# Seven places of split weights, 4128 bytes apart instead of 4096

## The chip, the core and the metric

One core of a Trainium2 chip runs the whole program. The metric is the device time of one execution in microseconds (us). Three executions of the kernel before took 2169.74, 2171.64 and 2173.57 us; the median, 2171.64 us, is the time to compare with.

## What is computed

Two transformer stacks in a row on 256 tokens of width 1024, all in float32. The first puts 16 meta tokens ahead (272 tokens) and has two layers of: half a SwiGLU feed-forward block (width 2816), a mixer (four retention heads and four differential attention heads) and another half feed-forward block. The second has two layers of feed-forward, mixer, feed-forward, where the mixer is a gated short convolution in layer 0 and dilated attention with three groups of 16 heads in layer 1. Cut to what matters here:

```python
h = h + 0.5 * (silu(rmsnorm(h) @ w_gate) * (rmsnorm(h) @ w_up)) @ w_down   # eight of these
h = h + mixer(rmsnorm(h) @ w_in) @ w_out                                    # four of these
```

Nearly all of the work is the product of a weight matrix, read once from memory, with activations of 256 or 272 columns (tokens).

## The kernel before

**Split products.** To keep float32 accuracy in TensorE's faster float32 format (fp32r), each operand is split in a high part, the value rounded to fp32r, and a low part, the difference. A product takes three matmuls: high weights by high activations, high weights by low activations, low weights by high activations. They are issued in the helper `matmuls` (L1658): the first at L1685, the second at L1686, the third at L1687. Where high and low activations lie one behind the other with 256 columns each (the feed-forward stages behind the first stack's second mixer), the first two are one matmul of 512 columns (L1683), and L1687 follows it. `project_first` (L1698, matmuls at L1702) does the same for the first six tiles. `values` (L2014, matmuls at L2025 to L2027) turns the roles round: the activations are the stationary operand, and the weights of three neighbouring places are the moving one, 3 by 128 columns.

**The weights' way.** SyncE's queue loads each unit of weights (L683, mostly 1024 rows by 256 columns) into one of four raw buffers, `raw`. ScalarE copies half a unit, [128 partitions, 8, 128], into a place of `whi` (L836, `highs`; the first six at L1152); VectorE subtracts this from the raw values into the same place of `wlo` (L1178, `lows`; the first six at L1636). Both tensors have seven places (`NP = 7`), and one place is 8 x 128 x 4 = 4096 bytes of every partition. `Plan` (L235) fixes ahead which tile of weights goes to which place: the one that was last used longest ago (L318), but for three neighbouring places kept for `values`. There are 728 tiles of weights. ScalarE fills a place again when the matmuls of its last tile are done (`plan.spent`), VectorE follows ScalarE (semaphore `hi`), and TensorE follows VectorE (`lo`, L1676). All this runs up to several tiles ahead.

**Where the operands lie.** The allocator puts the buffers of a partition one behind the other, each at a multiple of 32 bytes. `raw`, `whi`, `wlo`, `h` and `x` have sizes that are multiples of 256 bytes, so every place of `whi` and `wlo`, and the start of `x` and of `a`, is at the same byte mod 256; call it byte 0. Counted so, these are the starts of the moving operands:

| stages (index) | operand | columns | start, byte mod 256 |
|---|---|---|---|
| 0 to 3: feed-forward, mixer, feed-forward, feed-forward; 4: the tiles with 272 columns | `x`, `a` | 272 | 0 and 128 (high), 64 and 192 (low), by turns over k |
| 1: mixer, output | `y` | 272 | 32 and 96 to 224, by turns |
| 4: second mixer, query tiles | `x` from column 16 | 256 | 64 and 192 (high), 128 and 0 (low) |
| 5, 6, 8, 9, 11: feed-forward | `x_close`, `a_close` | 512 and 256 | 32 |
| 4 (output), 7, 10 | `y_close`, `x_close`, `c_yy`, `d_y` | 256 | 32 |

The 32 comes from `HALF_LINE = 8` elements in `close` (L552), and where that is 0, from what lies ahead of the buffer. One step over k inside a place is 128 x 4 = 512 bytes, two times 256.

The order of everything on the engines is written out by hand or by the plan; none of it depends on addresses.

Of the kernel before, what the change touches and what calls it, by code (L numbers as in the profile page):

```python
# [11 lines left out]
F32R = mybir.dt.float32r  # L12
# [3 lines left out]
P = 128  # L16
# [10 lines left out]
NP = 7  # L27
AHEAD = 6

HALF_LINE = 8  # L30
NH = 16
NSEG = 9

# [408 lines left out]
def build(nc, A, out):  # L442
    ctx = ExitStack()
    names = [0]

    def alloc(c, shape, dt=F32):
        names[0] += 1
        return c.enter_context(nc.sbuf_tensor(f"t{names[0]}", shape, dt))
# [3 lines left out]

    with ctx:
        raw = alloc(ctx, [P, NRAW, 8, PAIR])
        whi = alloc(ctx, [P, NP, 8, P], F32R)
        wlo = alloc(ctx, [P, NP, 8, P], F32R)
        h = alloc(ctx, [P, KC, T])
        x = alloc(ctx, [P, KC, 2, T], F32R)
        acc = alloc(ctx, [P, T])
# [19 lines left out]
        with block1:  # L479
# [4 lines left out]
            with region:  # L484
# [6 lines left out]
                rb = alloc(region, [33, 48])  # L491
                eb = alloc(region, [NH, NSEG * P])
                lam = alloc(region, [64, 16])
# [46 lines left out]
        ps = ctx.enter_context(nc.psum_tensor("ps", [P, 8, 512], F32))  # L540
        scr = nc.dram_tensor("bias_rows", [NH, NSEG * P], F32, kind="Internal")
        bands = nc.dram_tensor("bias_bands", [NH, P, 2, NKEY], F32, kind="Internal")

# [8 lines left out]
        def close(t, n, first):  # L552

            whole = t[:, :, :, :].rearrange("p k m c -> p (k m c)")
            return whole[:, first:first + n * 2 * SEQ].rearrange("p (k m c) -> p k m c", k=n, m=2)

        x_close, a_close, y_close = close(x, KC, HALF_LINE), close(a, FCH, HALF_LINE), close(y, KC, 0)

        raw_first = raw[:, 0:3, :, :].rearrange("p r k n -> p (r k n)").rearrange(
            "p (k u c) -> p k u c", k=KC, u=2)  # L560
# [130 lines left out]
        def _(pool):  # L691
# [21 lines left out]
            def mixer(s):  # L713
                l, cq = mix_of[s], STAGES[s][1]

                def rotate(kind, i, n):

                    c0, q = cq if kind in ("dq", "rq") else 0, 1 if kind in ("dq", "dk") else 0
                    v, row, turned = n % 2, ROW[kind] + i, sh[:, n % 2, 0:T - c0]
                    w.wait_ge(S["shuf"], 16 * l + n + 1)  # L720
                    pool.tensor_tensor(turned, turned, rotr[:, 2 * q + 1, c0:T], ALU.mult).then_inc(S["spun"], 1)
                    w.wait_ge(S["spun"], 16 * l + n + 1)
                    w.wait_ge(S["evac"], T0[s] + MIX_TILES.index((kind, i)) + 1)
                    pool.tensor_tensor(qk[:, row, c0:T], m1[:, v, 0:T - c0], turned, ALU.add).then_inc(S["qk"], 1)

                def low_y(kind, i, c):
                    w.wait_ge(*of_head("yh", l, kind, i))
                    hi, lo = (mixed_of(s)[:, c, m, 0:T - cq] for m in range(2))
                    pool.tensor_tensor(lo, yv[:, cq:T] if kind == "d" else qk[:, i, cq:T], f32(hi), ALU.subtract).then_inc(S["yl_" + kind], 1)

                def step(what, i):
                    if what == "O2":
                        low_y("d", i, 4 + i)
                    elif what == "R5":
                        low_y("r", i, i)

                n = 0
                for k, (kind, i) in enumerate(MIX_TILES):
                    if kind in ROW:
                        rotate(kind, i, n)  # L740
                        n += 1
                    for what, head in steps_at(k, True) + steps_at(k, False):
                        step(what, head)
                for n in sorted(OUT_STEPS):
                    for what, head in OUT_STEPS[n]:
                        step(what, head)
# [29 lines left out]
            mixer(plan.mixers[0])  # L776
            for n in range(NH):

# [11 lines left out]
            s = STAGES.index((DIL, META, W_FFN2 + 8))  # L790
            w.wait_ge(S["bands"], 16 * 8 * NH)

            w.wait_ge(S["evac"], T0[s])

            def bias(n):
                if n >= 2:
                    w.wait_ge(S["hmax"], n - 1)
                pool.dma_start(d_bias[:, n % 2, :, :], bands.ap()[n]).then_inc(S[f"bias{n % 2}"], 16)

            def stack_values(b):  # L800

                w.wait_ge(S["evac"], T0[s] + NT * b + NT)
                for half in range(2):
                    for g in range(2):
                        pool.dma_start(d_v12[64 * g:64 * g + 64, b % 2, half:4:2, :],
                                       d_vk[64 * half:64 * half + 64, b % 2, :, 1 + g, :]).then_inc(S["stacked"], 16)
# [3 lines left out]
            for b in range(KC):  # L810
                stack_values(b)
                for n in range(2 * b + 2, min(2 * b + 4, NH)):
                    bias(n)
# [1295 lines left out]
```

## Time and profile before

| | |
|---|---|
| median of three runs | 2171.64 us |
| the profiled execution: its time | 2173.17 us |
| the profiled execution: its span, first to last instruction | 2171.1 us |
| TensorE, matmuls | 2158.2 us busy (99%) |
| TensorE, weight loads (beside the matmuls) | 2039.8 us (94%) |
| VectorE | 1558.4 us (72%) |
| ScalarE | 1220.8 us (56%) |
| GpSimd | 458.1 us (21%) |
| DMA | 395.35 MB at a mean of 182 GB/s |

Busy time of TensorE counts a matmul from its start to its modelled end, and matmuls overlap. What sets the pace is the distance from one start to the next, and this has to be read from start times: over n starts, (last start - first start) / (n - 1).

### The profile page before, as it was taken

Reading aid. Unit: us, or ns where it says so; the run is one execution under the profiler, and the core shown is the slowest. Engines: PE = TensorE matmul, PEld = TensorE weight load, DVE = VectorE, ACT = ScalarE, POOL = GpSimd, SP = SyncE. Lnnn points to the kernel's source line nnn. Section 1 sums busy time; section 2 is a strip of 40 time slices with the busy share of each in tenths; the row PEclk is TensorE's granted clock in tenths of the full one; section 3 lists DMA queues with packets and bytes.
Section 4 is the critical chain, followed back from the end, with each engine's and each line's share of the span. In section 5 each row is a group of like instructions: output and inputs, shape, how many; then the busy total and the mean of one; then the engine's idle time right before and its main releaser. Section 6 shows DMA issues by size and latency. Waiting matters only on the chain.

```text
span 2171.1 us, 38708 instructions
## 1 busy us (share of the span) xinstructions
PE 2158.2 (99%) x15614; PEld 2039.8 (94%) x15614; DVE 1558.4 (72%) x2588; ACT 1220.8 (56%) x2017; POOL 458.1 (21%) x499
## 2 busy tenths in 40 slices
PE   9999999999999999999999999999999999999999
PEld 9999999999999999988988999889888999999888
DVE  8655977665665586876697586975876688887863
ACT  6444466444544456665566444655655576676652
POOL 1000522420350052231053000430331011101420
PEclk9999999999999999999999999999999999999999
DMA  8655435975786543565466554755555576674653
GB/s 279 206 165 174 152 118 147 240 191 166 197 208 183 174 156 117 172 198 194 155 213 204 186 185 147 230 193 192 181 190 177 168 198 173 175 230 141 225 178 106
DMA packets 424082, 395.35 MB, mean 182 GB/s; under 512 B 16816, under 2 KB 420400, under 8 KB 423905
## 3 DMA queue, kind: packets, MB, share of 16 engines
q1 hardware_dynamic: 410336, 375.22, 55.1%
q0 software_dynamic: 13280, 17.33, 3.8%
q8 instruction: 124, 2.03, 0.4%
q14 instruction: 54, 0.43, 0.1%
q10 hardware_dynamic: 288, 0.34, 0.0%
HBM read 389.20 MB, written 7.41 MB: 183 GB/s over the span
## 4 chain that ended last, share of the span: by engine, by line
PE 93%; DVE 3%; ACT 2%; DMA 1%; issue 1%; SPq 0%; ACTq 0%
PE ps L1687 29%; PE ps L1683 25%; PE ps L1685 16%; PE ps L1686 16%; DMA t<-attn_w_qkv 1%; DVE t L1178 1%; PE ps L2027 1%; PE ps L2026 1%; PE ps L2025 1%; PE ps L1702 1%; PE ps L1803 0%; PE ps L1848 0%; PE ps L1977 0%; DVE t L1213 0%; PE ps L1993 0%
## 5 line engine op out<-in xcount | busy, mean ns | idle before, releaser
L1687 PE MATMUL ps<-t 128*128 128x256 f32 (+1 forms) x5456 | 1548.2, 284 | 0.0
L1687 PEld LDWEIGHTS ps<-t 128*128 128x128 f32 x5456 | 1029.2, 189 | 0.1
L1178 DVE TENSOR_TENSOR t<-t 128x1024 fp32r<-128x1024 f32 (+1 forms) x722 | 876.4, 1231 | 174.5 <-ACT t L836 174.0
L1685 PE MATMUL ps<-t 128*128 128x272 f32 (+1 forms) x3036 | 876.2, 289 | 0.2 <-DVE t L1405 0.2
L836 ACT ACTIVATE t<-t 128x1024 fp32r<-128x1024 f32 (+1 forms) x722 | 729.9, 1030 | 256.7 <-PE ps L1687 229.1
L1686 PE MATMUL ps<-t 128*128 128x272 f32 (+1 forms) x3036 | 866.0, 285 | 0.0
L1683 PE MATMUL ps<-t 128*128 128x512 f32 x2420 | 840.2, 390 | 0.0
L1685 PEld LDWEIGHTS ps<-t 128*128 128x128 f32 x3036 | 571.5, 188 | 5.9 <-issue 3.4
L1686 PEld LDWEIGHTS ps<-t 128*128 128x128 f32 x3036 | 574.4, 189 | 0.9
L1683 PEld LDWEIGHTS ps<-t 128*128 128x128 f32 x2420 | 454.1, 188 | 95.0
L760 POOL TENSOR_TENSOR t<-t 128x256 f32<-128x256 f32 x110 | 100.6, 914 | 694.2 <-ACT t L954 694.2
L944 ACT ACTIVATE t<-ps 128x256 f32<-128x256 f32 x220 | 83.1, 378 | 132.4 <-PE ps L1687 132.4
L783 POOL DMA_DIRECT2D bias_bands<-bias_rows x128 | 104.2, 821 | 217.3 <-PE ps L1687 165.3
L753 POOL TENSOR_TENSOR t<-t 128x256 fp32r<-128x256 f32 x110 | 129.6, 1178 | 9.4 <-ACT t L937 9.4
L851 ACT ACTIVATE t<-t 128x256 fp32r<-128x256 f32 (+1 forms) x95 | 49.7, 531 | 91.8 <-DVE t L1263 83.2
L974 ACT ACTIVATE t<-t 128x272 fp32r<-128x272 f32 x66 | 28.5, 432 | 115.5 <-DVE t L1358 115.5
L1213 DVE SCALAR_TENSOR_TENSOR t<-ps,t 128x512 f32<-128x512 f32 (+2 forms) x52 | 28.6, 551 | 80.4 <-ACT t L879 80.1
L937 ACT ACTIVATE t<-t 128x256 fp32r<-128x256 f32 x110 | 45.6, 415 | 66.9 <-DVE t L1328 66.9
L1324 DVE TENSOR_TENSOR t<-ps,t 128x256 f32<-128x256 f32 x110 | 46.7, 424 | 48.9 <-ACT t L944 45.8
L1317 DVE TENSOR_TENSOR t<-ps,t 128x256 f32<-128x256 f32 x110 | 46.2, 420 | 43.6 <-ACT t L944 42.9
L1328 DVE TENSOR_TENSOR t<-t 128x256 f32<-128x256 f32 x110 | 71.0, 645 | 0.0
L1355 DVE TENSOR_TENSOR t<-ps,t 128x272 f32<-128x272 f32 x66 | 29.1, 440 | 50.7 <-PE ps L1687 50.7
(200 smaller groups left out, 1560.1 us busy)
## 6 DMA issues: line engine op xcount, KB each, us to landing
t<-ffn_w_in SPq DMA_DIRECT2D x88, 1024.0 KB, 5.3
t<-ffn_w_gate SPq DMA_DIRECT2D x42, 1024.0 KB, 5.5
t<-ffn_w_up SPq DMA_DIRECT2D x42, 1024.0 KB, 7.4
t<-attn_w_qkv SPq DMA_DIRECT2D x72, 512.0 KB, 4.8
t<-ffn_w_down SPq DMA_DIRECT2D x32, 1024.0 KB, 5.2
t<-ffn_w_out SPq DMA_DIRECT2D x32, 1024.0 KB, 5.3
t<-w_in SPq DMA_DIRECT2D x28, 1024.0 KB, 5.0
t<-ffn_w_down SPq DMA_DIRECT2D x16, 768.0 KB, 4.4
```

The source lines that it names most:

```text
L753: pool.tensor_tensor(a_close[:, j, 1, :], us[:, j % 2, 0:SEQ], f32(a_close[:, j, 0, :]), ALU.subtract).then_inc(S["al"], 1)
L760: pool.tensor_tensor(sl[:, j % 2, 0:SEQ], sl[:, j % 2, 0:SEQ], rstd[:, META:T], ALU.mult).then_inc(S["factor"], 1)
L783: pool.dma_start(bands.ap()[n, 64 * r:64 * r + 64, q, c:end].rearrange("i (k j) -> k i j", j=64), bass.AP(scr, n * NSEG * P + seg * P + 63 ...
L836: act.activation(whi[:, plan.place[n], 0:nk, :], kept(u)[:, 0:nk, half * P:half * P + P], ACT.Copy).then_inc(S["hi"], 1)
L851: act.activation(placed(e, parts_of(e)[:, m, 0, 0:T - c0]), hm, ACT.Copy, scale=gain(e, m)).then_inc(S["xh"], 1)
L944: act.activation(part[:, m, :], ps[:, plan.bank[t], SEQ:2 * SEQ], ACT.Copy).then_inc(S["part"], 1)
L1178: dve.tensor_tensor(wlo[:, plan.place[n], 0:nk, :], kept(u)[:, 0:nk, half * P:half * P + P], f32(whi[:, plan.place[n], 0:nk, :]), ALU.subt ...
L1328: dve.tensor_tensor(us[:, i, 0:N], us[:, i, 0:N], sl[:, i, 0:N], ALU.mult).then_inc(S["prod"], 1)
L1683: pe.matmul(ps[:, r.banks[j], :].rearrange("p (m n) -> p m n", m=2), hi, both(k), start=i == 0, stop=False)
L1685: pe.matmul(o, hi, xhi, start=i == 0, stop=False)
L1686: pe.matmul(o, hi, xlo, start=False, stop=False)
L1687: ins = pe.matmul(o, lo, xhi, start=False, stop=i == r.nk - 1)
```

## The change

Each place gets 32 bytes more: `PLACE` = 1032 elements = 4128 bytes, of which 4096 are used as before. Place p begins at byte 32p mod 256: 0, 32, 64, 96, 128, 160, 192 for the seven. `whi` and `wlo` are now views of two flat tensors; these are 7 x 1032 + 8 = 7232 elements, 256 bytes longer than before each, so everything allocated behind them moves by 512 bytes and keeps its byte mod 256. `raw` lies ahead of both and stays.

```diff
 HALF_LINE = 8
+PLACE = 8 * P + HALF_LINE
...
-        whi = alloc(ctx, [P, NP, 8, P], F32R)
-        wlo = alloc(ctx, [P, NP, 8, P], F32R)
+        whi_all = alloc(ctx, [P, NP * PLACE + HALF_LINE], F32R)
+        wlo_all = alloc(ctx, [P, NP * PLACE + HALF_LINE], F32R)
...
+        whi, wlo = (t[:, 0:NP * PLACE].rearrange("p (n c) -> p n c", n=NP)[:, :, 0:8 * P].rearrange(
+            "p n (k c) -> p n k c", k=8) for t in (whi_all, wlo_all))
```

No instruction, wait or transfer is added, removed or moved. Only the addresses of the seven places change, for those who write them (L836, L1152, L1178, L1636) and those who read them (L1178, L1636 and the matmuls).

## Rows read from the trace of the kernel before

**Rows 1.** The page: busy time by engine, and TensorE's granted clock in 40 slices.

```profile
PE 2158.2 (99%) x15614; PEld 2039.8 (94%) x15614; DVE 1558.4 (72%) x2588; ACT 1220.8 (56%) x2017; POOL 458.1 (21%) x499
...
PEclk9999999999999999999999999999999999999999
```

**Rows 2.** Groups of TensorE's matmuls by line and shape: busy us, mean ns.

```profile
L1687 PE MATMUL ps<-t 128*128 128x256 f32 x3504 | 984.9, 281 | 0.0
L1683 PE MATMUL ps<-t 128*128 128x512 f32 x2420 | 840.2, 390 | 0.0
L1685 PE MATMUL ps<-t 128*128 128x272 f32 x1952 | 568.7, 291 | 0.0
...
L1685 PE MATMUL ps<-t 128*128 128x256 f32 x1084 | 307.5, 284 | 0.2 <-DVE t L1405 0.2
...
L2025 PE MATMUL ps<-t 128*128 128x384 f32 x128 | 43.0, 336 | 0.0
```

**Rows 3.** L1683, 900 to 1000 us: count, duration min/median/max, first and last start.

```profile
L1683 PE MATMUL ps<-t x290: 390/390/390, 899.7 to 999.9; 128*128 128x512 f32 x145
```

**Rows 4.** The same of L1687 in stage 7, 1270 to 1320 us.

```profile
L1687 PE MATMUL ps<-t x144: 277/279/280, 1269.9 to 1319.9; 128*128 128x256 f32 x144
```

**Rows 5.** The same of L1687 in stage 3, 570 to 690 us.

```profile
L1687 PE MATMUL ps<-t x319: 286/287/290, 570.0 to 689.8; 128*128 128x272 f32 x160
```

**Rows 6.** Timeline, stage 4, first and last matmul of a 24-matmul tile: start, length.

```profile
795.56 0.28 PE L1685 MATMUL ps<-t 128*128 128x256 f32 x1
...
798.27 0.28 PE L1687 MATMUL ps<-t 128*128 128x256 f32 x1
```

**Rows 7.** Timeline, stage 10, first and last matmul of a 24-matmul tile.

```profile
1741.32 0.28 PE L1685 MATMUL ps<-t 128*128 128x256 f32 x1
...
1744.02 0.28 PE L1687 MATMUL ps<-t 128*128 128x256 f32 x1
```

**Rows 8.** Waits of TensorE's matmuls: us in total, times, longest.

```profile
PE ps L1848 <- ACT t L1012: 2.3, 2, 1.2
...
PE ps L1685 <- DVE t L1405: 0.2, 1, 0.2
```

**Rows 9.** Weight loads of transposes: min/median/max ns of two lines; then merged on the timeline.

```profile
L1829 PEld LDWEIGHTS ps<-t x24: 138/140/143, 232.9 to 831.9; 128*128 128x128 f32 x24
```

```profile
L1993 PEld LDWEIGHTS ps<-t x96: 138/140/143, 1746.9 to 1967.2; 128*128 128x128 f32 x96
```

```profile
251.51 0.49 PE L1829 MATMUL ps<-t 128*128 128x128 f32 x3
```

```profile
1746.97 1.04 PE L1993 MATMUL ps<-t 128*128 128x128 f32 x8
```

**Rows 10.** Timeline, stage 10, `values`: the first and last of 15 matmuls in a row.

```profile
1761.32 0.34 PE L2025 MATMUL ps<-t 128*128 128x384 f32 x1
...
1763.75 0.34 PE L2027 MATMUL ps<-t 128*128 128x384 f32 x1
```

**Rows 11.** Groups of VectorE and ScalarE by line and shape.

```profile
L1178 DVE TENSOR_TENSOR t<-t 128x1024 fp32r<-128x1024 f32 x658 | 819.4, 1258 | 174.5 <-ACT t L836 174.0
```

```profile
L836 ACT ACTIVATE t<-t 128x1024 fp32r<-128x1024 f32 x658 | 681.2, 1050 | 256.7 <-PE ps L1687 229.1 <-DMA t<-attn_w_qkv 21.9 <-DMA t<-ffn_w_up 3.6
...
L937 ACT ACTIVATE t<-t 128x256 fp32r<-128x256 f32 x110 | 45.6, 415 | 66.9 <-DVE t L1328 66.9
...
L851 ACT ACTIVATE t<-t 128x256 fp32r<-128x256 f32 x56 | 29.9, 542 | 49.4 <-DVE t L1263 40.9 <-DVE t L1261 8.5
L974 ACT ACTIVATE t<-t 128x272 fp32r<-128x272 f32 x66 | 28.5, 432 | 115.5 <-DVE t L1358 115.5
...
L851 ACT ACTIVATE t<-t 128x272 fp32r<-128x272 f32 x39 | 19.8, 514 | 42.3 <-DVE t L1263 42.3
```

**Rows 12.** The page: the chain that ended last, by line.

```profile
PE ps L1687 29%; PE ps L1683 25%; PE ps L1685 16%; PE ps L1686 16%; DMA t<-attn_w_qkv 1%; DVE t L1178 1%; PE ps L2027 1%; PE ps L2026 1%; PE ps L2025 1%; PE ps L1702 1%; PE ps L1803 0%; PE ps L1848 0%; PE ps L1977 0%; DVE t L1213 0%; PE ps L1993 0%
```

## The prediction

> **What bounds the kernel now.** I read four views, in this order. First the page's busy shares: TensorE's matmuls cover 99% of the span at a granted clock that stands at its upper level, 2.4 GHz, in every slice; VectorE has 72%, ScalarE 56% [rows 1]. Then the groups by shape, to see what TensorE does: 2420 pairs of a 512-column and a 256-column matmul, 1952 triples of 272 columns, 3504 - 2420 = 1084 triples of 256 columns, and 128 triples of 384 columns, whose moving operand is the weights [rows 2]. Third the waits: the matmuls' largest entry is 2.3 us in total, over the whole span, and the main line's is 0.2 us [rows 8]. Nothing starves TensorE. Last, because a matmul's shown length overlaps its neighbours', the distances between starts:
>
> - pairs: (999.9 - 899.7) / 289 = 346.7 ns for 768 columns [rows 3];
> - 256-column triples in stage 7: (1319.9 - 1269.9) / 143 = 349.7 ns for 768 columns [rows 4];
> - 272-column triples: (689.8 - 570.0) / 318 = 376.7 ns for 816 columns [rows 5].
>
> At one column per cycle of 2.4 GHz these would be 320, 320 and 340 ns. So each step has some 27 to 37 ns on top, 8 to 11%, and this sum over all steps is the only thing in this kernel that addresses could touch with effect: 2420 x 26.7 + 1084 x 29.7 + 1952 x 36.7 = 168 us. The question of this change is whether any of it depends on where the weights begin.
>
> **The change, part by part.**
>
> *Matmuls that load their weights from a place (L1683 to L1687, L1702).* Same instructions, other start bytes for six places of seven. What do the rows say of start bytes? Before the change the weights always begin at byte 0 and only the moving operand varies. Pairs and stage 7's triples have it at byte 32 [rows 3, 4]. Stage 4's query tiles have the same shape as stage 7's, with starts at 64, 128, 192 and 0: 23 distances in 798.27 - 795.56 = 2.71 us, 117.8 ns each, 353.5 per triple against 349.7 [rows 4, 6]. That is 3.8 ns a triple, 1.1%, and the only row that shows anything like an effect of an address. But stage 10 has byte 32 throughout, and one of its tiles takes 1744.02 - 1741.32 = 2.70 us, 352.2 a triple [rows 7]. So 2.5 of the 3.8 ns appear with no change of address, behind stages that are interrupted by other work; I read them as a rhythm in which the stream settles. For the stationary side itself two lines serve: L1829 loads from `vt` at multiples of 64, L1993 from `d_p`, which by the allocator's count begins at byte 96, a half of 64 further. Both loads last 138/140/143 ns, and the distances are (0.49 - 0.27) / 2 = 0.11 us and (1.04 - 0.27) / 7 = 0.11 us [rows 9]. These matmuls have only 128 columns, 53 ns of streaming, so the 110 ns are the load's own pace; it is the same at either start. And in `values` the stationary operand (`x_close`) is at byte 32 and the moving one (the weights) at 0: (1763.75 - 1761.32) / 14 = 173.6 ns for 384 columns, 1.085 of the bare 160 [rows 10], as near to the pairs' 346.7 / 320 = 1.083 as the rounding lets one see. With the roles of bytes 0 and 32 exchanged the rate stays. I take 0 ns. The bounds are 3.8 ns a step to the worse, and to the better 6.7 ns for a 272-column triple (worked out below).
>
> *`values` (L2025 to L2027).* Three pieces of 512 bytes, now 4128 apart. 384 matmuls; bounded by a third of 3.8 ns each, 0.5 us, up or down; 0 taken, since they run at the pairs' rate.
>
> *Writers and the reader beside them (L836, L1152, L1178, L1636).* 730 operations on each engine. ScalarE's writes to `a_close`, at byte 32, take 415 ns for 256 columns, and to `a`, at byte 0, 432 ns for 272: 17 ns for 16 columns, nothing left for the start. L851's means say otherwise, 542 for 256 columns at byte 32 against 514 for 272 at 0, so at worst 28 + 17 = 45 ns an operation [rows 11]. 730 x 45 = 33 us more on ScalarE, 56% busy becoming 58%; VectorE likewise, 72% to 74%. The cover is that both run tiles ahead, and ScalarE even waits 229 us at L836 for TensorE to free a place [rows 11]. What is not covered is what stands in the chain: VectorE's L1178 with 1% of the span, 22 us [rows 12]; 45 / 1258 of this is 0.8 us. A gain has no way to the end, since TensorE doesn't wait. I take 0.3, range 0 to 0.8.
>
> *Buffers behind.* They move by 512 bytes, so keep their byte mod 256: 0. No DMA, wait or queue entry changes; the loads go to `raw`, which stays.
>
> **Sum.** The profiled execution took 2173.17 us, 2.1 more than its span; plus 0 + 0 + 0.3 it is 2173.5. That execution stood 1.5 us above the median, 2171.64, so for a median I say 2172.0. A measurement of this kernel can tell about 0.2%, 4.3 us, from no change. If this case holds, I expect 2168 to 2176.
>
> **A rule against the trace.** The rows show 116.6 ns from start to start for 256 columns in stage 7 [rows 4]. The Trainium skill, "TensorE: Matmul & The Clock Gate", section "Back-to-back issue gap", gives the isolated gap as N / 2.4 plus about 2.5 ns, 109.2 here; the trace disagrees by 7.4 ns. The same page, in "Step-by-step: what each phase is for", says that loading the next weights takes no read bandwidth from the running matmul, as the two have ports of their own. By that second rule the start of the weights can't matter, and the time stays; by the first, something unnamed costs 7 ns a matmul, and this is what rival 4 lets the change remove.
>
> **Rivals.**
>
> 1. *Slower: weights and stream must stand 32 bytes apart.* Suppose that the 3.8 ns between stage 4 and stage 7 come from the distance between the weights' start and the stream's. Then every step with the stream at byte 32 loses them at six places of seven: the pairs (2420) and the 256-column triples outside stage 4's query tiles (1084 - 96 = 988), 3408 x 6/7 x 3.8 = 11.1 us, 2183. The 272-column steps already go through four distances and stay. It decides for slower from 1.5 ns a step on (4.3 / 2921). For it: the gap between stages 4 and 7. Against: rows 7, 9 and 10 as read above; and the pairs' length is 390/390/390 over all seven places [rows 3], so there is no jitter that a clash with others would bring. Chance 0.26.
>
> 2. *Faster: the 272-column steps gain.* Their excess is 1.108 of bare against 1.093 for stage 7. If the distance 0 or 64 costs this, the change gives many steps other distances. The best case is stage 7's 116.6 plus 16 columns, 6.7 ns, 123.3 a matmul against 125.6: 2.3 x 3 x 1952 = 13.5 us, at six places of seven 11.5: 2160. Against: byte 0 to 192 already occur by turns in these steps, so most of the gain would have to come from odd places alone. Chance 0.12.
>
> 3. *The change does less than it says.* If only the byte mod 64 counts, places 0, 2, 4 and 6 are as before and three of seven differ: 3408 x 3/7 x 3.8 = 5.5 us slower, or 5.8 faster by rival 2's price. Chance 0.06, half to each side.
>
> 4. *The whole excess is an address clash* and leaves six places of seven: 168 x 6/7 = 144 us, 2028. Nothing but its size speaks for it; the stationary starts of rows 9 and 10 speak against. Chance 0.01.
>
> **How the numbers follow.** No effect: 0.55, the likeliest, 2172.0. Faster by over 0.2%: 0.12 + 0.03 + 0.01 = 0.16. Slower: 0.26 + 0.03 = 0.29. The range reaches up to rival 1 with the writers' 0.8 and the runs' own 2 us, 2186, and down to 2163, between rivals 3 and 2, where 0.08 is left out below and about as much above.
>
> **What would show it.** Right: the pairs' distance stays at 346.7 ns in every stage and place; 349.7 in stage 7; 376.7 in stages 0, 2 and 3; stages 4 and 10 may settle in other rhythms between 350 and 354. Rival 1: the same stretches stay near 346.7 at place 0 and grow elsewhere, with the 512-column length leaving 390. Rival 2: 272-column distances fall while the pairs stand. Rival 3: odd places differ from even ones. L836 near 1050 and L1178 near 1258 ns, or up to 45 more at most. My forecast is wrong if any of the three steady distances moves by more than 1.5 ns a step, or if TensorE begins to wait at L1685 for VectorE.

## The result, and the profile after

| | before | after |
|---|---|---|
| median of the runs compared | 2171.22 us (2169.74 to 2173.57, 4 runs) | 2182.47 us (2182.09 to 2182.94, 4 runs) |
| the profiled execution: time, span | 2173.17, 2171.1 us | 2182.53, 2180.4 us |

The changed kernel is slower: the ratio is 1.0052, with a 95% interval of 1.0040 to 1.0064. That is 11.3 us. The line numbers of the engines' code are 4 higher than before.

Busy time of the changed kernel, from its page, with the granted clock; they answer to [rows 1]:

```profile
PE 2168.2 (99%) x15614; PEld 2039.0 (94%) x15614; DVE 1555.3 (71%) x2588; ACT 1221.3 (56%) x2017; POOL 454.6 (21%) x499
...
PEclk9999999999999999999999999999999999999999
```

TensorE has 10 us more to do with as many instructions, at the upper level of the clock as before; VectorE and ScalarE have what they had. Which matmuls grew is seen in the groups by shape (the answer to [rows 2]; columns: busy us, mean ns):

```profile
L1691 PE MATMUL ps<-t 128*128 128x256 f32 x3504 | 984.1, 281 | 0.0
L1687 PE MATMUL ps<-t 128*128 128x512 f32 x2420 | 849.6, 395 | 0.0
L1689 PE MATMUL ps<-t 128*128 128x272 f32 x1952 | 567.7, 291 | 0.0
```

The 512-column matmul went from 390 to 395 ns; the others show nothing in their lengths. The distances between starts show more. These rows are the same stretches as [rows 3], [rows 4] and [rows 5]: count, duration min/median/max, first and last start.

```profile
L1687 PE MATMUL ps<-t x285: 387/395/423, 899.9 to 999.7; 128*128 128x512 f32 x143
```

```profile
L1691 PE MATMUL ps<-t x142: 277/281/286, 1269.7 to 1319.8; 128*128 128x256 f32 x142
```

```profile
L1691 PE MATMUL ps<-t x319: 283/288/297, 570.0 to 689.7; 128*128 128x272 f32 x160
```

Pairs: 99.8 / 284 = 351.4 ns (346.7 before). Stage 7's triples: 50.1 / 141 = 355.3 (349.7). 272-column triples: 119.7 / 318 = 376.4 (376.7). The 512-column lengths, which were 390/390/390, now spread from 387 to 423.

In stage 7, tile by tile, the places differ. Below are the first and last of the 24 matmuls of three tiles, at places 0, 1 and 6, from the timeline: start, length.

```profile
1293.66 0.28 PE L1689 MATMUL ps<-t 128*128 128x256 f32 x1
...
1296.34 0.28 PE L1691 MATMUL ps<-t 128*128 128x256 f32 x1
```

```profile
1276.58 0.28 PE L1689 MATMUL ps<-t 128*128 128x256 f32 x1
...
1279.34 0.28 PE L1691 MATMUL ps<-t 128*128 128x256 f32 x1
```

```profile
1290.78 0.29 PE L1689 MATMUL ps<-t 128*128 128x256 f32 x1
...
1293.54 0.28 PE L1691 MATMUL ps<-t 128*128 128x256 f32 x1
```

23 distances in 2.68, 2.76 and 2.76 us: 349.6, 360.0 and 360.0 ns a triple. Place 0, whose address did not change, runs as before; places 1 and 6 lose 3%. The four tiles at places 2 to 5 that lie between these take 352 to 355.

The pairs differ by place too. Over all uninterrupted single tiles of the feed-forward projections, from the first 512-column start of a tile to its eighth, places 0 to 6 take 346.7, 352.6, 352.4, 351.3, 347.4, 351.5 and 355.8 ns a pair, in each tile of a place the same within 1 ns. Here are the first and the eighth of a tile at place 1:

```profile
952.59 0.40 PE L1687 MATMUL ps<-t 128*128 128x512 f32 x1
...
955.05 0.40 PE L1687 MATMUL ps<-t 128*128 128x512 f32 x1
```

2.46 us / 7 = 351.4 ns to the 0.01 us that the rows show, 352.6 by the trace's own times.

The waits have not moved (answer to [rows 8]), and the writers' lengths neither (answer to [rows 11]), so the loss is in no queue and in no other engine:

```profile
PE ps L1852 <- ACT t L1016: 2.2, 2, 1.2
...
PE ps L1689 <- DVE t L1409: 0.2, 1, 0.2
```

```profile
L1182 DVE TENSOR_TENSOR t<-t 128x1024 fp32r<-128x1024 f32 x658 | 818.0, 1255 | 174.4 <-ACT t L840 174.0
```

```profile
L840 ACT ACTIVATE t<-t 128x1024 fp32r<-128x1024 f32 x658 | 681.7, 1050 | 257.8 <-PE ps L1691 231.8 <-DMA t<-attn_w_qkv 20.0 <-DMA t<-ffn_w_up 4.0
```

The spans of the stages, each from its first matmul of a weight tile to the next stage's, worked out from the start times of the two traces:

| | before | after | difference |
|---|---|---|---|
| stages 0 to 4 (mostly 272 columns) | 875.70 | 873.75 | -1.95 |
| stages 5, 6, 8, 9, 11 (pairs) | 921.04 | 931.40 | +10.36 |
| stage 7 | 89.84 | 91.06 | +1.22 |
| stage 10 | 279.27 | 278.77 | -0.50 |

With 0.2 us more ahead of the first tile the sum is the 9.3 us between the spans. Of the -1.95, 1.79 are in stage 0: it took 204.93 us in this execution of the kernel before and 202.1 to 203.8 in every other trace of this study, so they are that execution's start and no gain. 9.3 + 1.8 = 11.1 us, close to the 11.3 between the medians.

### The profile page after: what moved, and what is told of

The parts are those of the page before. It is cut to its first block, busy times and chain, and to the rows that moved or that the text cites. A ratio compares the mean times of both kernels' runs of the same rounds, so it can differ in the third digit from the quotient of the medians.

```text
span 2180.4 us, 38708 instructions
## 1 busy us (share of the span) xinstructions
PE 2168.2 (99%) x15614; PEld 2039.0 (94%) x15614; DVE 1555.3 (71%) x2588; ACT 1221.3 (56%) x2017; POOL 454.6 (21%) x499
## 4 chain that ended last, share of the span: by engine, by line
PE 94%; DVE 2%; ACT 2%; DMA 1%; issue 1%; SPq 0%; ACTq 0%
PE ps L1691 29%; PE ps L1687 26%; PE ps L1689 16%; PE ps L1690 16%; DMA t<-attn_w_qkv 1%; PE ps L2031 1%; PE ps L2029 1%; PE ps L2030 1%; DVE t L1182 1%; PE ps L1706 1%; PE ps L1807 0%; PE ps L1852 0%; PE ps L1981 0%; PE ps L1997 0%; PE ps L2010 0%
## 5 line engine op out<-in xcount | busy, mean ns | idle before, releaser
L1687 PE MATMUL ps<-t 128*128 128x512 f32 x2420 | 849.6, 395 | 0.0
L1687 PEld LDWEIGHTS ps<-t 128*128 128x128 f32 x2420 | 454.4, 188 | 106.3
L1359 DVE TENSOR_TENSOR t<-ps,t 128x272 f32<-128x272 f32 x66 | 29.0, 439 | 50.1 <-PE ps L1691 50.1
```

The lines of the kernel that those rows point to most:

```text
L1687: pe.matmul(ps[:, r.banks[j], :].rearrange("p (m n) -> p m n", m=2), hi, both(k), start=i == 0, stop=False)
```

## The experiments

In all of them "distance" is the byte at which the stream (the moving operand) starts less the byte at which the weights start, mod 256. The kernel before has 32 for all pairs and 256-column triples outside stage 4's queries; the changed kernel has 32 - 32p for place p. A step is one pair or one triple. The ns are means over the whole trace, of steps that no other work interrupts, from start times; the rows shown repeat some of them.

### All weights 32 bytes on, all places alike

```diff
+PLACE = 1024
...
-        whi = alloc(ctx, [P, NP, 8, P], F32R)
-        wlo = alloc(ctx, [P, NP, 8, P], F32R)
+        alloc(ctx, [P, 8])
+        whi_all = alloc(ctx, [P, NP * PLACE], F32R)
+        wlo_all = alloc(ctx, [P, NP * PLACE], F32R)
+        alloc(ctx, [P, 56])
```

The flat tensors have the size of those before, and `whi` and `wlo` are views of them. The 8 elements ahead are the 32 bytes; the 56 behind make it 256, so that all that follows keeps its byte.

The theories that the expectations name by letters: D, the distance counts; C, only a change of start from place to place costs; W, the weights' own byte counts; H, only the byte mod 64 counts; A, each load has its own price by its distance; R, the stream settles in a rhythm; P, the level of the whole program differs.

> All places 4096 bytes apart again, but all of them begin 32 bytes later than in the kernel before, at byte 32, where the streams of the pairs and 256-column triples begin too; everything else keeps its byte mod 256. Theory D (distance): what counts is the stream's start less the weights' start, mod 256. Then every place is what place 1 was in the changed kernel: stage 7 at 358.5 ns a triple, pairs at about 352, so 988 x 8.5 + 2420 x 5.5 = 21.7 us slower than before, about 2193 us. Theory C (change of place): only a start that differs from place to place costs; a common one does not: 2171 us. Theory W (the weights' own byte): weights off byte 0 are slow wherever the stream is: slower, as much as D says.

Measured: 2176.87 us, 1.0029 (1.0018 to 1.0040). First the pairs, then stage 7 (count, duration min/median/max, first and last start):

```profile
L1689 PE MATMUL ps<-t x260: 390/391/392, 899.9 to 989.7; 128*128 128x512 f32 x130
```

```profile
L1693 PE MATMUL ps<-t x126: 283/283/284, 1275.0 to 1320.0; 128*128 128x256 f32 x126
```

Stage 7 takes 45.0 / 125 = 360.0 ns a triple at every place: for triples D holds and C falls. But the pairs take 89.8 / 259 = 346.7 ns, nothing more than before, where D had 352, and the 272-column triples 375.0, 1.7 less. So D's 21.7 us did not come: 988 x 10 - 1952 x 1.7 = 6.6 us; measured 6.2.

One distance, two rates: at distance 0 the pairs of the changed kernel's place 1 took 352.6 ns, and here 346.7. The steps show how. In place 1 of the changed kernel they go 350, 350, 361 over and over; here the first run of each of the five stages, four tiles by turns, goes so too (352.9 ns, 346.8 in the kernel before), and then the single tiles settle at 346.7. In both kernels the tile at place 1 has the same starts mod 256 throughout its 16 matmuls, so what a pair costs at distance 0 depends on more than those; what ran ahead of it is the nearest reading. The distance alone does not explain the pairs' loss at place 1.

### Weights and all that follows 32 bytes on

```diff
-        whi = alloc(ctx, [P, NP, 8, P], F32R)
-        wlo = alloc(ctx, [P, NP, 8, P], F32R)
+        alloc(ctx, [P, 8])
+        whi_all = alloc(ctx, [P, NP * PLACE], F32R)
+        wlo_all = alloc(ctx, [P, NP * PLACE], F32R)
```

> Places 4096 bytes apart, and the weights and everything allocated behind them 32 bytes later, so weights at byte 32, streams at 64, distance 32 as in the kernel before. Only the raw buffers stay. D: as before, 2171 us, pairs at 346.7, stage 7 at 349.7 ns. C: the same. W: slower by about 22 us, as in the run beside it, since the weights are at byte 32 in both.

Measured: 2170.08 us, 0.9999 (0.9989 to 1.0009). Pairs, then stage 7:

```profile
L1688 PE MATMUL ps<-t x260: 389/390/391, 899.9 to 989.7; 128*128 128x512 f32 x130
```

```profile
L1692 PE MATMUL ps<-t x129: 277/278/281, 1274.9 to 1319.7; 128*128 128x256 f32 x129
```

346.7 and 44.8 / 128 = 350.0 ns, as before. The weights are at byte 32 here as in the run above, and triples that took 360 there take 350: it is not the weights' own byte (W falls), it is where the stream stands to them.

### All weights 64 bytes on

As the first, with `[P, 16]` ahead and `[P, 48]` behind: distance -32.

> As the first of these runs, but the weights 64 bytes later, distance -32. D (mod 256): every place is what place 2 was: stage 7 near 354.5, pairs near 352.5 ns: 2420 x 5.8 + 988 x 4.8 = 18.8 us slower than before, 2190 us. H (only the byte mod 64 counts): distance -32 is distance 32 mod 64, so as before, 2171 us. C: 2171 us.

Measured: 2189.56 us, 1.0089 (1.0074 to 1.0104), as D said. The pairs:

```profile
L1689 PE MATMUL ps<-t x255: 391/402/403, 899.9 to 989.7; 128*128 128x512 f32 x128
```

89.8 / 254 = 353.5 ns, and by the mean of all, 353.3; stage 7 355.0. Distances 32 and -32 are the same mod 64 and differ by 1.9% in the pairs, so H falls. And here the pairs pay although all places are alike, so C falls for them too at this distance.

### Places 64 bytes further apart

```diff
+PLACE = 1040
...
+        whi_all = alloc(ctx, [P, NP * PLACE], F32R)
+        alloc(ctx, [P, 16])
+        wlo_all = alloc(ctx, [P, NP * PLACE], F32R)
+        alloc(ctx, [P, 16])
```

> The places 4160 bytes apart, so they begin at bytes 0, 64, 128, 192, 0, 64, 128. H: mod 64 all are alike, as before, 2171 us. D (mod 256): places 0 and 4 cost nothing, 1 and 5 what place 2 cost, 2 and 6 what place 4 did (352.7 in stage 7), 3 what place 6 did (358.9): the mean over seven places is 3.4 ns a step, 3408 x 3.4 = 11.6 us, 2183 us. C: slower than before as the change was, about 2182.

Measured: 2177.53 us, 1.0033 (1.0020 to 1.0046): slower, so against H, but only 6.8 us where D's sum had 11.6. Over the single tiles of stage 7, from first to last start, places 0 to 6 take 350.0, 355.2, 356.3, 359.6, 350.2, 355.3 and 357.1 ns a triple. Places 0 and 4, at distance 32, again cost nothing. But places 2 and 6 have the distance -96 of the changed kernel's place 4, which took 352.0, and of the four tiles at place 6 one takes 360.3, the others 355.7 to 356.3. A price per distance is close, but not the whole of it.

### High and low parts apart

Four kernels with `PLACE = 1024` and the parts begun at different bytes; the lead ahead of `whi` and the gap between `whi` and `wlo`, in elements, were 8 and 56; 0 and 8; 16 and 48; 0 and 16, and what follows kept its byte.

> Only the high parts begin at byte 32; the low parts stay at byte 0, as in the kernel before. In a triple, two of the three loads are of high parts, in a pair one of two. Theory A (each load has its own price by its distance): stage 7 at 350 + 2/3 x 10 = 356.7 ns; pairs stay at 346.7, as they did with both at 32. About 988 x 6.7 = 6.6 us over before, less what the 272-column steps gain (up to 1.7 ns each, 3 us): 2174 to 2178. Theory R (a rhythm of the whole stream): no such share; stage 7 at 350 or at 360, or lower than both because successive loads differ, as they did where the changed kernel took places 2 and 3 by turns (343.2 ns a pair).

> Only the low parts begin at byte 32. A: stage 7 at 353.3 ns, pairs at 346.7; 988 x 3.3 = 3.3 us over before, less what the 272-column steps gain: 2171 to 2174. R: 350 or 360, or under 350.

> Only the high parts begin at byte 64. With both there, pairs took 353.3 and stage 7 355.0 ns. A: a pair loads its high part while the 256-column matmul ahead streams, and if that load pays, the pairs take up to 353.3 and stage 7 353.3: up to 16.0 + 3.3 us over before, 2190. If it is the low part's load, beside the 512 columns, that pays, the pairs stay at 346.7: 2174. R: neither, a value of its own, possibly under 346.7.

> Only the low parts begin at byte 64. A: the complement of the run beside it: the pairs' surcharges of the two sum to 6.7 ns, stage 7's to 5.0 ns (here 1.7). R: they don't sum.

Measured, beside the runs with one start for both (272 columns: the projections of stages 0, 2 and 3 alone). The kernel before had a median of 2171.3 us beside the last four and of 2170.7 beside the two above them; each ratio is to its own:

| high, low at byte | pairs, ns | stage 7, ns | 272 columns, ns | median, us | ratio (95%) |
|---|---|---|---|---|---|
| 0, 0 (before) | 346.7 | 350.0 | 376.7 | 2171.3 | |
| 32, 32 | 346.7 | 360.0 | 375.0 | 2176.87 | 1.0029 (1.0018 to 1.0040) |
| 64, 64 | 353.3 | 355.0 | 376.7 | 2189.56 | 1.0089 (1.0074 to 1.0104) |
| 32, 0 | 353.3 | 353.3 | 373.5 | 2186.68 | 1.0070 (1.0055 to 1.0085) |
| 0, 32 | 344 to 353 | 356 | 373.6 | 2173.96 | 1.0013 (1.0004 to 1.0023) |
| 64, 0 | 346.7 | 354.7 | 373.4 | 2170.01 | 0.9994 (0.9985 to 1.0004) |
| 0, 64 | 348.9 | 353.3 | 374.6 | 2176.37 | 1.0023 (1.0013 to 1.0033) |

A falls. With both at 32 the pairs pay nothing, with the high parts alone 6.7 ns; the surcharges of 64, 0 and of 0, 64 sum to 2.2 where the two together cost 6.7. So loads have no prices that add, and a step's time depends on more than its own starts. The kernel with only the low parts at 32 shows this best: three rates for the same code at the same addresses mod 256. Its pairs in stages 5, 6 and 9:

```profile
L1689 PE MATMUL ps<-t x256: 398/398/398, 899.7 to 989.8; 128*128 128x512 f32 x128
```

```profile
L1689 PE MATMUL ps<-t x260: 391/391/391, 1089.9 to 1179.7; 128*128 128x512 f32 x130
```

```profile
L1689 PE MATMUL ps<-t x263: 387/389/389, 1539.6 to 1629.9; 128*128 128x512 f32 x132
```

90.1 / 255 = 353.3, 89.8 / 259 = 346.7 and 90.3 / 262 = 344.7 ns. Each rate holds through its stage, 8 and 11 are like 5, and the lengths (398, 391, 387 to 389) show which one it is. Its ten executions ran from 2169.27 to 2178.87 us, wider than any other kernel's here. So the addresses allow several steady rhythms, and what came ahead of the stage seems to pick one, as in the pairs at distance 0 above; this is read from traces, and no run was made to test it.

### High parts at 64 where 272 columns follow

```diff
+                        if r.c0[j] == 0:
+                            self.off[n] = (16, 0)
...
-                    hi, lo = (wt[:, plan.place[piece], k % 8, :] for wt in (whi, wlo))
+                    hi, lo = (of(piece)[:, k % 8, :] for of in (high_of, low_of))
```

A tile with `c0` = 0 meets 272 columns (the first six tiles are left as they were); its offsets are in elements, for the high and the low part. `high_of(n)` is the place of tile n from its offset on; places are 4352 bytes apart (17 x 256), so that each has slack of its own.

> The high parts begin at byte 64 only for tiles that meet 272 columns (in slack of their own inside each place); all other tiles lie as in the kernel before. If the distance sets the rhythm step by step (theory D, with R for the rhythm), the 272-column steps run as they did with all high parts at 64, 373.5 ns against 376.7, and the pairs and 256-column triples as before: 1952 x 3.1 = 6.1 us faster than before, about 2165 us. Theory P (the level of the whole program, its memory or its weights' transfers, explains the differences): no change, 2171.

Measured: 2165.45 us, 0.9973 (0.9962 to 0.9983). The 272-column triples, then the pairs:

```profile
L1706 PE MATMUL ps<-t x309: 282/288/288, 569.9 to 684.9; 128*128 128x272 f32 x155
```

```profile
L1702 PE MATMUL ps<-t x261: 390/390/390, 899.7 to 989.8; 128*128 128x512 f32 x131
```

115.0 / 308 = 373.4 ns, and 90.1 / 260 = 346.5. D and R as foretold; P falls. The places now alternate between bytes 0 and 256 mod 512, and the pairs and stage 7 take what they took, so a shift by 256 bytes changes nothing in them.

### The streams by turns

```diff
+                first = 48 + 1088 * (k // 2) if k % 2 == 0 else 568 + 1088 * (k // 2)
+                return x_flat[:, first:first + 2 * SEQ].rearrange("p (m c) -> p m c", m=2)[:, m, cols]
```

The weights are those of the kernel before; this is where the activations of chunk k lie in `x` for stages 5, 6, 8, 9 and 11.

> The weights stay at byte 0; in the projections of the five feed-forward stages with pairs, the stream begins at byte 192 for even k and 224 for odd k, distances -64 and -32 by turns. In the changed kernel, two tiles taken by turns from places 3 and 2 had these distances, and ran at 343.2 ns a pair. D and R: the same here although now the streams moved and not the weights: 1600 pairs of single tiles at 343.2 in place of 346.7, 5.6 us faster than before, 2165.5 us. If it was the weights' own bytes 64 and 96, or the change of place, that gave 343.2: 346.7 or above, up to 353, 2171 to 2182.

Measured: 2165.85 us, 0.9973 (0.9964 to 0.9982). The pairs:

```profile
L1695 PE MATMUL ps<-t x264: 390/391/392, 899.7 to 990.0; 128*128 128x512 f32 x132
```

90.3 / 263 = 343.3 ns, the rate that the changed kernel had reached at places 2 and 3. There the weights had moved, here the streams: with the run that moved both by 32 bytes, the strongest sign for the distance. The first runs of four tiles do not gain (349.7 ns, 346.8 before).

### Both, and the outputs' weights by turns

The two edits above, and this:

```diff
+                        if STAGES[s][:2] == (FFN, META) and r.nk == FCH and r is not runs[-1]:
+                            self.off[n] = (16 + 8 * j, 16 + 8 * j)
```

> Both edits of the two runs beside it, and in the feed-forward outputs that are taken as two tiles by turns, one tile's parts at byte 64 and the other's at 96: 660 pairs at 343.2 in place of 346.7, 2.3 us. D and R: 6.1 + 5.6 + 2.3 = 14 us faster than before, about 2157 us.

Measured: 2167.98 us, 0.9985 (0.9977 to 0.9994), 11 us off what was foretold. The pairs of stage 5's output:

```profile
L1716 PE MATMUL ps<-t x40: 397/400/402, 1029.6 to 1043.5; 128*128 128x512 f32 x40
```

13.9 / 39 = 356.4 ns instead of 343.2; by the mean of all, 356.6 over 660 pairs, 6.5 us lost where 2.3 were to be won. The projections kept 343.3. Six runs of two tiles in the changed kernel had the same distances in the same order at 343.2. What tells them apart is open: the pitch of the places, or the rhythm that the stream came with.

### Two of the three

> The two edits that each took about 5 us off, without the third, which made the feed-forward outputs' pairs take 356.6 ns. They touch different steps, so D says that they add: 272-column steps at 373.5, single-tile pairs at 343.3, all else as before; 6.1 + 5.2 us faster than before, 2160 us. If some fixed amount is lost as soon as TensorE runs ahead (weights come too late), less: 2163 to 2166.

Measured: 2161.14 us (2161.07 to 2162.79, 5 runs), 0.9955 (0.9942 to 0.9969), 9.9 us under the kernel before. The 272-column triples, the pairs and stage 7:

```profile
L1718 PE MATMUL ps<-t x309: 282/288/288, 569.8 to 684.8; 128*128 128x272 f32 x155
```

```profile
L1714 PE MATMUL ps<-t x264: 390/392/392, 899.6 to 989.9; 128*128 128x512 f32 x132
```

```profile
L1718 PE MATMUL ps<-t x129: 277/278/281, 1274.9 to 1319.7; 128*128 128x256 f32 x129
```

373.4, 343.3 and 350.0 ns. The two gains alone were 5.4 and 5.0 us and add up to 10.4; 9.9 came. It beats both kernels, and in it a tile's start goes by the columns that it meets, not by its place.

## Why the prediction was right or wrong

**The likeliest case failed, rival 1 came.** No effect, at 0.55, did not come; the measured 2182.47 us lies in the range and beside rival 1's 2183, which had 0.26. By the prediction's own signs: pairs moved by 4.7 ns and stage 7 by 5.6, both over its 1.5; place 0 stayed.

**The step that failed** is the first part of the sum, "I take 0 ns" for the matmuls' weights. It set aside the one row that showed an effect of addresses, stage 4 against stage 7 (in the trace's own times, the steps of [rows 6]'s tile run from 348 to 363 ns, those of stage 7 stay at 350), because of three others:

- Stage 10's 352.2 at distance 32 [rows 7] was read as a rhythm, and that holds. Below are, in the kernel before, the first and the last of the 96 matmuls of four whole tiles in a row, first in stage 4's output and then in stage 10's, with the same lines, shape and distance: 11.08 and 11.18 us for 95 distances, 349.9 and 353.1 ns a triple. But it does not follow that the distance is without effect: moving it moved the rates.

```profile
869.74 0.28 PE L1685 MATMUL ps<-t 128*128 128x256 f32 x1
...
880.82 0.28 PE L1687 MATMUL ps<-t 128*128 128x256 f32 x1
```

```profile
1973.28 0.28 PE L1685 MATMUL ps<-t 128*128 128x256 f32 x1
...
1984.46 0.28 PE L1687 MATMUL ps<-t 128*128 128x256 f32 x1
```

- The loads of L1829 and L1993 [rows 9] compare loads that set the pace themselves, each beside a short stream. They speak of a load's own start, which indeed costs nothing (the run with weights and all that follows 32 bytes on), but not of a load against a stream. By the kernel's sizes `d_p` begins at byte 224 mod 256, not 96; that too is 32 beyond a multiple of 64, so the comparison stands.
- `values` with the roles exchanged [rows 10] kept its rate, and was taken for all shapes. It answers little: 521.8 ns a triple before, 522.2 with weights at 32, 523.4 at 64, and 526.0 at most, with the high parts alone at 64. That is 0.8%, where the pairs and the 256-column triples answered with up to 2.9%.

**Rival 1's terms.** Its mechanism, the distance between stream and weights, is what the first three runs show, and the streams by turns; the rhythm that comes on top was not in it. Its price was one for all: 3.8 ns a step at six places. Measured were 10.36 us / 2420 = 4.3 ns for a pair, with the last triples of these stages in it, 1.22 / 256 = 4.8 for stage 7's triples, and stage 10 no slower as a whole though its projections' uninterrupted triples rose from 351.6 to 356.0 ns (its span differs by more than that among kernels in which all its starts are as before: 276.9 to 279.3 us). That the sum, 11.1 us, met 11.3 is partly luck. Its picture that only distance 32 is good is wrong: pairs with all places at distance 0 run at 346.7, and by turns at -64 and -32 faster than at 32. And its price, one for all, stands for losses between 0.7 and 9.5 ns by place.

**The other steps.** Writers: 1050 and 1255 ns, so 0 where 0.3 was taken. Buffers behind: 0, right. `values`: 520.8 against 521.8 ns, within its bound. No wait changed. Rival 2 was wrong for this change (376.4 against 376.7), though a gain for 272 columns exists, 3.2 ns with the high parts at 64; its bound was 6.7. Rival 3 falls with the run at 64 bytes. Rival 4 falls: no run took more than 3.4 of the pairs' 26.7 ns away.

## What to carry to other kernels

Where matmuls follow each other without a gap and each loads new weights, the byte at which the stream starts less the byte at which the weights start, mod 256, is a tuning knob worth from -1% to +3% of a step here. Start with the same for all buffers of a ring (pairs at distance 0 lost 6 ns only where the places differed), then vary it on purpose, per shape, and measure each choice: prices per distance don't add. Read it from start times over some hundred matmuls, not from shown lengths, and beware of a row of another shape as a proxy.

## What the hardware showed that was not expected

- Triples of 256 columns take 350.0, 353.3, 354.7, 355.0, 356 or 360.0 ns in stage 7, pairs 343.3 to 356.6, where nothing but starts was changed, at the upper level of the clock.
- The Trainium skill, "TensorE: Matmul & The Clock Gate", section "Step-by-step: what each phase is for", says that loading the next weights takes no read bandwidth from the running matmul. From this alone the starts would not matter, and here they do: with everything else equal, moving the weights by 32 bytes against the stream made 256-column triples 10 ns (2.9%) longer. Whether read bandwidth is what they share was not tried.
- The same code at the same addresses mod 256 ran at 344.7, 346.7 and 353.3 ns a pair in different stages of one execution, each rate kept for a whole stage; and pairs at distance 0 took 352.6 ns in one kernel and 346.7 in another.
